# Stick-breaking attention of a two-layer decoder step: suffix sums in plain fp32 and the diagonal mask added by VectorE

## What is computed

```python
z = jnp.einsum('bqhd,bkhd->bhqk', q[:, i0:i0 + blk], kb) * scale + bias_f
mask = jnp.arange(end)[None, :] < qpos[:, None]
log_fail = jnp.where(mask, jax.nn.log_sigmoid(-z), 0.0)
after = lax.cumsum(log_fail, axis=3, reverse=True) - log_fail
w = jnp.where(mask, jnp.exp(jax.nn.log_sigmoid(z) + after), 0.0)
outs.append(jnp.einsum('bhqk,bkhd->bqhd', w, vb))
```

## Time and profile before

| What | Value |
|---|---|
| Median of three runs (lowest, highest) | 1834.61 us (1832.61, 1837.99) |
| Profiled execution: its own time | 1834.27 us |
| Its span, first to last instruction | 1832.5 us |
| TensorE busy | 1617.6 us, 88% of the span |
| TensorE weight loads | 1250.3 us, 68% |
| VectorE, ScalarE, GpSimd busy | 753.0, 627.7, 566.6 us |
| Mean granted clock of TensorE | 0.908 of full speed |

### The profile page before, as it was taken

The page is one execution under the profiler, slowest core; times in us unless marked ns, Lnnn a source line. Parts: engine busy times, 40 slices in busy tenths (PEclk is TensorE's granted clock), DMA queues, the critical chain, the costliest instruction groups (busy, mean ns, idle before and its releaser), DMA issues.

```text
span 1832.5 us, 25351 instructions
## 1 busy us (share of the span) xinstructions
PE 1617.6 (88%) x9409; PEld 1250.3 (68%) x9409; DVE 753.0 (41%) x1039; ACT 627.7 (34%) x1069; POOL 566.6 (31%) x472
## 2 busy tenths in 40 slices
PE   5689998875887999999989867999879899999997
PEld 3467665553655666666766545665559899999996
DVE  2650004135486576766656683003341421221121
ACT  3312225222233331433324232235532442342341
POOL 1221221000232333333323333332303344444443
PEclk9788999667998999999989988995789999999999
DMA  7564997732455879888996967631003232332332
GB/s 245 184 234 133 295 326 235 249 116 81 139 174 159 252 268 332 272 274 275 317 314 206 316 234 229 220 126 46 1 1 92 67 94 81 91 92 86 92 90 77
DMA packets 288755, 325.96 MB, mean 178 GB/s; under 512 B 13814, under 2 KB 205952, under 8 KB 288436
## 3 DMA queue, kind: packets, MB, share of 16 engines
q1 hardware_dynamic: 286312, 316.56, 53.9%
q0 software_dynamic: 2320, 7.78, 1.1%
HBM read 315.48 MB, written 8.99 MB: 177 GB/s over the span
## 4 chain that ended last, share of the span: by engine, by line
PE 68%; DVE 11%; DMA 6%; SPq 5%; issue 4%; ACT 4%; POOL 1%; DVEq 0%; ACTq 0%; POOLq 0%
PE PS L477 43%; PE PS L491 4%; DMA wring<-w_ffn_up 3%; PE PS L516 3%; SPq L1210 3%; PE PS L436 2%; DVE prod L2244 2%; PE PS L1000 2%; PE PS L786 2%; PE PS L426 1%; SPq L1206 1%; DVE scr L2249 1%; DVE scr L1970 1%; DMA vring<-cache_sb_v 1%; PE PS L534 1%
## 5 line engine op out<-in xcount | busy, mean ns | idle before, releaser
L1340 POOL TENSOR_TENSOR parts<-wring,parts 128x512 fp32r<-128x512 f32 (+1 forms) x400 | 518.3, 1298 | 1146.5 <-ACT parts L1418 1145.8
L477 PE MATMUL PS<-hh_r,parts 128*128 128x260 f32 (+1 forms) x2880 | 722.1, 340 | 48.4 <-POOL parts L1340 27.1
L477 PEld LDWEIGHTS PS<-hh_r,parts 128*128 128x128 f32 x2880 | 497.4, 192 | 140.5 <-issue 83.3
L1418 ACT ACTIVATE parts<-wring 128x512 fp32r<-128x512 f32 (+1 forms) x400 | 247.2, 622 | 876.4 <-PE PS L477 683.5
L477 PE MATMUL PS<-hl_r,parts 128*128 128x260 f32 (+1 forms) x1440 | 464.6, 335 | 0.0
L477 PEld LDWEIGHTS PS<-hl_r,parts 128*128 128x128 f32 x1440 | 277.2, 192 | 27.8 <-issue 1.7
L477 PE MATMUL PS<-E_r,parts 128*128 128x260 f32 (+1 forms) x1584 | 265.2, 327 | 6.5 <-POOL parts L1340 3.9
L477 PEld LDWEIGHTS PS<-E_r,parts 128*128 128x128 f32 x1584 | 230.2, 192 | 45.8 <-issue 22.2
L2244 DVE TENSOR_TENSOR prod<-kring,PS 128x1024 f32<-128x1024 f32 x128 | 150.1, 1213 | 23.4 <-DMA kring<-cache_sb_k 23.4
L2249 DVE TENSOR_REDUCE scr<-prod 128x16 f32<-128x1024 f32 x128 | 149.7, 1211 | 0.0
L2426 DVE TENSOR_TENSOR xT<-xT,PS 128x512 f32<-128x512 f32 (+1 forms) x64 | 44.1, 689 | 207.5 <-PE PS L477 207.5
(11 more groups left out here) (313 smaller groups left out, 1545.0 us busy)
## 6 DMA issues: line engine op xcount, KB each, us to landing
vring<-cache_sb_v SPq DMA_DIRECT2D x256, 256.0 KB, 4.2
kring<-cache_sb_k SPq DMA_DIRECT2D x256, 256.0 KB, 3.7
wring<-w_ffn_up SPq DMA_DIRECT2D x88, 512.0 KB, 5.4
wring<-w_ffn_down SPq DMA_DIRECT2D x16, 1024.0 KB, 6.2
kring<-w_ffn_up SPq DMA_DIRECT2D x12, 1024.0 KB, 9.9
vring<-w_ffn_up SPq DMA_DIRECT2D x10, 1024.0 KB, 10.3
wring<-w_mem_kv SPq DMA_DIRECT2D x8, 1024.0 KB, 8.2
wring<-w_in_gla SPq DMA_DIRECT2D x8, 1024.0 KB, 11.3
```

The lines of the kernel that those rows point to most:

```text
L477: last = mm(PS[:, bank + c, 0:w], parts[:, q, a, P * k:P * k + P], x[:, k0 + kk, o:o + w], start=(q == 0 and k == 0 and a == 0 and x is sr ...
L1340: gp.tensor_tensor(part_as(n, 1, src, w), src, part_as(n, 0, src, w), ALU.subtract).then_inc(wlo_ok, 1)
L1418: return fn(dst, src, ACT.Copy)
```

## The change

The sums take softplus as it stands, in plain fp32, with the fp32 constants `tri` and `ones`: ten products per head in place of twenty, and no high and low part, so `high`, the GpSimd subtractions, `sb_constants`' copies and the semaphores between them go. `sbt` has four buffers where it had two; ScalarE's passes of head h wait for the sum of head h - 4 (`r_done`) in place of the low part of h - 2. The four mask products per head go; in their place VectorE adds `later` (the same -2^100) to the diagonal blocks in `sbz`, in two instructions of two blocks each, behind the eviction of the same head. ScalarE's passes now wait for these (`sbc_ok`, counted per head), and so does VectorE's addition; the next head's scores still wait for the eviction alone (`z_read`). GpSimd's `sb_stores` keeps the two transfers of keys and values to HBM.

```diff
@@ layer 1's buffers
-        sbt = [ringF[:, SBW * p:SBW * p + SBW] for p in range(2)]
-        sb_hi, sb_lo = ([ringR[:, SBW * (a + p):SBW * (a + p) + SBW] for p in range(2)] for a in (2, 4))
-        identR, onesR, triR, laterR = (ringR[:, 6 * SBW + P * k:6 * SBW + P * k + P] for k in range(4))
+        sbt = [ringF[:, SBW * p:SBW * p + SBW] for p in range(4)]
@@ TensorE, scores and suffix_sums
-                        mm(PSf[:, SBO[kc]:SBO[kc] + w], zT[r:r + 64, 4 + j, P * kc:P * kc + P],
-                           zT[r:r + 64, j, P * kc:SEQ], start=True, stop=False)
-                        last = mm(PSf[:, SBO[kc]:SBO[kc] + P], identR, laterR, start=False, stop=True)
+                        last = mm(PSf[:, SBO[kc]:SBO[kc] + w], zT[r:r + 64, 4 + j, P * kc:P * kc + P],
+                                  zT[r:r + 64, j, P * kc:SEQ], start=True, stop=True)
...
-                    pe.wait_ge(splo_ok, h + 1)
+                    x = sbt[h % 4]
+                    pe.wait_ge(spr_ok, h + 1)
...
-                        for x in parts_:
-                            last = mm(PSf[:, o:o + w], triR, x[:, SBO[kc]:SBO[kc] + w], start=(x is parts_[0]),
-                                      stop=(kc == TT - 1 and x is parts_[1]))
+                        last = mm(PSf[:, o:o + w], tri[:, :], x[:, SBO[kc]:SBO[kc] + w], start=True, stop=(kc == TT - 1))
...
-                            for x in parts_:
-                                last = mm(PSf[:, o + P * (k2 - kc):o + P * (k2 - kc) + w2], onesR,
-                                          x[:, SBO[k2]:SBO[k2] + w2], start=False, stop=(k2 == TT - 1 and x is parts_[1]))
+                            last = mm(PSf[:, o + P * (k2 - kc):o + P * (k2 - kc) + w2], ones[:, :],
+                                      x[:, SBO[k2]:SBO[k2] + w2], start=False, stop=(k2 == TT - 1))
...
-                pe.wait_ge(sbc_ok, 1)
@@ GpSimd, sb_lows (now sb_stores)
-                for h in range(SBH):
-                    pool.wait_ge(sphi_ok, h + 1)
-                    gp.tensor_tensor(sb_lo[h % 2], sbt[h % 2], sb_hi[h % 2], ALU.subtract).then_inc(splo_ok, 1)
@@ ScalarE
-                for dst, src in ((identR, ident), (laterR, later), (triR, tri), (onesR, ones)):
-                    last = copy(dst, src[:, :])
-                last.then_inc(sbc_ok, 1)
...
-                    act.wait_ge(z_read, h + 1)
-                    if h >= 2:
-                        act.wait_ge(splo_ok, h - 1)
-                    abs_exp_ln(sbt[h % 2], sbz[h % 4], zl_ok)
-
-                def high(h):
-                    act.wait_ge(spr_ok, h + 1)
-                    if h >= 2:
-                        act.wait_ge(r_done, h - 1)
-                    copy(sb_hi[h % 2], sbt[h % 2]).then_inc(sphi_ok, 1)
+                    act.wait_ge(sbc_ok, h + 1)
+                    if h >= 4:
+                        act.wait_ge(r_done, h - 3)
+                    abs_exp_ln(sbt[h % 4], sbz[h % 4], zl_ok)
@@ VectorE, evict and softplus
+                    dve.wait_ge(z_read, h + 1)
+                    for o, n in ((0, 512), (896, 128)):
+                        blocks = sbz[h % 4][:, o:o + 2 * n].rearrange("p (a n) -> p a n", a=2)[:, :, 0:P]
+                        last = tt(blocks, blocks, later[:, :].rearrange("p (a n) -> p a n", a=1).to_broadcast((P, 2, P)), ALU.add)
+                    last.then_inc(sbc_ok, 1)
...
-                    dve.wait_ge(z_read, h + 1)
+                    dve.wait_ge(sbc_ok, h + 1)
```

More of the change, by code:

```diff
@@ L322, in build @@
         ge_ok, acthi_ok, act_ok, tail_st, z_done, z_read, zl_ok, spr_ok = (sem(n) for n in ("ge_ok", "acthi_ok", "act_ok", "tail_st", "z_done", "z_read", "zl_ok", "spr_ok"))
-        sphi_ok, r_done, zr_ok, splo_ok, w_ok, sbo_done, sbhi_ok, kt_st = (sem(n) for n in ("sphi_ok", "r_done", "zr_ok", "splo_ok", "w_ok", "sbo_done", "sbhi_ok", "kt_st"))
+        r_done, zr_ok, w_ok, sbo_done, sbhi_ok, kt_st = (sem(n) for n in ("r_done", "zr_ok", "w_ok", "sbo_done", "sbhi_ok", "kt_st"))
         y_st, state_st, s_rcopy, s_sum_done, s_ev, s_sq, s_r, s_h = (sem(n) for n in ("y_st", "state_st", "s_rcopy", "s_sum_done", "s_ev", "s_sq", "s_r", "s_h"))
@@ L999, in scores @@
                         w = SEQ - P * kc
-                        mm(PSf[:, SBO[kc]:SBO[kc] + w], zT[r:r + 64, 4 + j, P * kc:P * kc + P],
-                           zT[r:r + 64, j, P * kc:SEQ], start=True, stop=False)
-                        last = mm(PSf[:, SBO[kc]:SBO[kc] + P], identR, laterR, start=False, stop=True)
+                        last = mm(PSf[:, SBO[kc]:SBO[kc] + w], zT[r:r + 64, 4 + j, P * kc:P * kc + P],
+                                  zT[r:r + 64, j, P * kc:SEQ], start=True, stop=True)
                     last.then_inc(z_done, 1)
                 def suffix_sums(h):
-                    pe.wait_ge(splo_ok, h + 1)
+                    x = sbt[h % 4]
+                    pe.wait_ge(spr_ok, h + 1)
                     if h:
                         pe.wait_ge(zr_ok, h)
-                    parts_ = (sb_hi[h % 2], sb_lo[h % 2])
                     for kc in range(TT):
@@ L1349, in gla_masks, with sb_stores @@
                        channel_multiplier=1).then_inc(att_ok, 1)
-            def sb_lows():
+            def sb_stores():
                 flat = lambda ap: ap.rearrange("t h d -> t (h d)")
@@ L1368, in _ @@
                         else:
-                            sb_lows()
+                            sb_stores()
                 if j == 6:
@@ L1871, in sb_prompt @@
                 key_rows(0)
-                high(0)
                 key_rows(2)
@@ L1875, in sb_prompt @@
                 for h in range(SBH):
-                    if h + 1 < SBH:
-                        high(h + 1)
                     if h and h % 2 == 0:
@@ L2531, in evict @@
                     ts(sbz[h % 4], PSf[:, 0:SBW], SBD ** -0.5, sbb[:, h:h + 1], ALU.mult, ALU.add).then_inc(z_read, 1)
+                    dve.wait_ge(z_read, h + 1)
[3 more added lines that the diff above has]
+                    last.then_inc(sbc_ok, 1)
                 def softplus(h):
-                    dve.wait_ge(z_read, h + 1)
+                    dve.wait_ge(sbc_ok, h + 1)
                     dve.wait_ge(zl_ok, h + 1)
-                    stt(sbt[h % 2], sbz[h % 4], 0.0, sbt[h % 2], ALU.max, ALU.add).then_inc(spr_ok, 1)
+                    stt(sbt[h % 4], sbz[h % 4], 0.0, sbt[h % 4], ALU.max, ALU.add).then_inc(spr_ok, 1)
                 def token_low(j):
```

## The result

The changed kernel takes 1814.76 us (median of four runs, 1809.19 to 1821.22) against 1836.3 us before in the same comparison (four runs, 1832.61 to 1842.77): a ratio of 0.9876, 95% interval 0.9846 to 0.9905, so between 17 and 28 us less. The forecast was 14.9 us less. The unchanged file, run again later in another comparison, gave 1809.77 us and 0.9856 (0.9829 to 0.9883).

The account below looks back on a forecast made before the run. TensorE, 68% of the chain of waits, was taken as the bound, its prices set by the granted clock. Layer 1's attention: -7.7 - 8.3 + 1.1 = -14.9 us, from 1834.27 to about 1819.4 us; range 1812 to 1831 us.

Parts of the forecast that it names:

- Score price: Layer 1's attention: one head's scores without mask products cost 5.5 us at 1.2 GHz, about 2.9 us at 2.4 GHz.
- Front: Layer 1's attention up to the first suffix sum, 27.70 us before: 7.7 us less.
- Now it needs only the last copy of the projection: First score's start in layer 1's attention: no wait for ScalarE's four fp32r constant copies, 2.1 us saved.
- head 0's path: Scores, eviction, mask, ScalarE's passes and VectorE's addition before the first sum: ready near 1246.3 us, before TensorE at 1249.3 us.
- Body: Middle of layer 1's attention, TensorE nearly always busy: 52.2 us against 60.5 us, 8.3 us less, scores and sums mostly at 2.4 GHz.
- The two waits: TensorE's waits ahead of the values, for VectorE's subtraction and an exponential on ScalarE: estimated 0.35 us each, 0.7 us together.
- Their removal gains nothing in the body: Later heads' high and low parts lay beside TensorE's work, so dropping them was said to gain nothing there.
- Tail: End of layer 1's attention, behind sum 5: 25.9 us against 24.8 us, 1.1 us more, with 3.3 us of waiting.
- the end that was chosen: VectorE's mask: low end, 0.42 us per addition, 0.85 us per head; the upper end was 3.1 us.
- The first: Rival: scores pull the clock down every time; body 1.0 us more, 1829 us in all, no measurable change; chance 0.12.
- The second: Rival: plain fp32 sums do not lift the clock, 8.9 us per sum; 1867 us in all, slower; chance 0.07.
- The third: Rival: clock high from the first score on, as TensorE never rests; 32 us less, 1802 us in all; chance 0.03.

Follow-up runs that it names:

- the last version but one: Changed kernel with ScalarE's copy of the first key rows moved ahead of head 0's three passes: 1803.84 us, ratio 0.9834.

## Why the prediction was right, and where its sizes were off

Faster it was, and the first median lies in the range, 4.6 us below the forecast; the second median, 1809.77 us, lies 2 us below the range. By stage, 7.7, 8.3 and -1.1 us were forecast and 11.7, 14.1 and -0.1 us came. That the first median fell into the range is partly luck: the low end, 1812 us, is 22.3 us below the profiled 1834.27 us, and the stage alone gave 25.7 us. The direction, and the high clock under scores and sums, came as forecast; the prices below did not.

**Score price: mis-sized.** The step took a score as 7.10 us less four mask products at their own 0.40 us, 5.5 us, and 2.9 us at the high clock. Measured: 4.56 and 2.36 us. A mask product's row does not hold what it does to its neighbours; leaving the masks out showed it. For five scores of the body that is 2.7 us.

**Front: the start was wrong in two ways that partly cancel.** "Now it needs only the last copy of the projection" was taken as 2.1 us, with all three scores at 1.2 GHz. Without the wait the first two ran at 2.4 GHz: together with the new score price they were 2.40, 2.42 and 4.56 us in place of 16.5 us, 7.1 us less, and the transposes 0.5 us less. Against it stand waits of 0.62 and 2.94 us that the forecast did not have. It asked what is late next for the sum and followed head 0's path to the sum; the key transposes, which wait on the same ScalarE, were left out. In all it took 15.99 us against 20 us.

**Body: the clock as chosen, and the values better.** Scores and sums at 2.4 GHz were right (0.97; a sum 4.53 us, forecast 4.45 us). The values, left at 4.0 us, took 2.38 us, since in this run the scores without masks no longer cost the clock ahead of them: 3.2 us. Sum 0 took 5.73 us for 6.7 us: only its first product and the start of the second were cold, that is at 1.2 GHz. The two waits were 0.72 and 0.71 us, twice the estimate of 0.35 us. Together 46.40 us in place of 52.2 us.

**"Their removal gains nothing in the body": true of before, not of the change.** Alone, the sums bring nothing that can be told. With the masks gone, the high and low parts would have been the bound: keeping them costs 7.8 us of the attention.

**Tail: as forecast in kind.** The wait was 3.07 us (forecast 3.3), the sums 4.74 and 4.54 us (4.45), the values 3.80 and 4.09 us (4.1 and 4.56). VectorE's additions took 0.42 us, the end that was chosen.

**The rivals.** The first does not hold: no score in the body of either profile of the changed kernel pulled the clock down. The second does not hold: plain fp32 lifted the clock in the body even with masks (0.89). The third was nearer than its chance of 0.03 said. Its condition, a high clock from the first score on, was missing here by one wait; with the wait moved it was met throughout front and body, and the front came out as worked out for it (11.22 us, forecast 10.9 us). The attention got shorter by 32.0 us, as much as its three stages added up to, but by errors that cancel: the body was 3.4 us shorter than worked out (45.17 us, 48.6 us) and the tail 2.9 us longer (24.52 us, 21.6 us).

The Trainium skill's page "TensorE: Matmul & The Clock Gate", section "Why this matters for your kernels", also asks for no long idle gap between bursts of products. Here that half agrees in kind: the clock was at 1.00 ahead of the wait of 2.94 us and at 0.50 behind it. The length of a wait did not settle it alone: behind 2.17 us the scores had 0.50, and behind 3.07 us, in the second profile, the values had 1.00. Being busy alone was not enough either, with 8.79 us of 8.79 us busy at 0.50.

Open is what it is in the masked scores that loses the clock: their shape, their length, or the stalls of the weight loads. No run separated these. Open too is why scores without masks hold the high clock but did not bring it back (4.58 us of 4.58 us busy at 0.50 with the masks left out). That the additions on VectorE cost nothing beyond their time was not run by itself either.

## What to carry to other kernels

Price a small instruction between others by taking it out, not by its own row alone. A wait ahead of TensorE can cost its length again in the clock of what follows, so the order of the other engines at a stage's start is worth a look once TensorE gets there earlier. An edit that gains nothing by itself may gain on top of another: here the sums alone changed the median by less than can be told, the masks moved alone (with the first wait gone) took 18.0 us off it, and both together 24.5 us.

## What was not expected of the hardware

- Score products over 64 rows keep 2.4 GHz behind full-row work: in the last version but one the granted clock is 1.00 for the whole front, though TensorE was busy for only 9.37 of 11.30 us; behind a wait of 2.17 us the same products had 0.50 while busy for 4.60 of 4.60 us.
- A full-row mask product of 128 columns between 64-row products cost 0.63 us at 1.2 GHz, 0.40 us of it in its own row; at 2.4 GHz (3.96 - 2.36) / 4 = 0.40 us, 0.26 us of it in its own row.
- At 2.4 GHz a sum over 2560 columns in plain fp32 took 4.53 us, and the same sum in fp32r, run twice over the columns, 2.92 us.
